# Seven half-size block products in place of eight, for 18 of 22 tile pairs of two up projections

## What is computed

```python
h = x
h = h + 0.5 * swiglu(rms_norm(h, ffn1_norm), w_gate1, w_up1, w_down1)     # FFN 1, "plain"
h = h + mixer(rms_norm(h, mix_norm))          # sparse attention and retention
h = h + 0.5 * swiglu(rms_norm(h, ffn2_norm), w_gate2, w_up2, w_down2)     # FFN 2, "plain"
h = rms_norm(h + sigmoid(rms_norm(h, ple_norm) @ w_ple_gate) * (p @ w_ple_proj), final_norm)
h = h + gated_linear_attention(rms_norm(h, ...))
h = h + conv_ffn(rms_norm(h, ...))            # FFN 3, with a convolution
out = rms_norm(h, final_norm_2)

def swiglu(x, w_gate, w_up, w_down):
    return (silu(x @ w_gate) * (x @ w_up)) @ w_down
```

## Time and profile before

| | us |
|---|---|
| median of 3 runs | 1851.72 (1851.65 to 1852.01) |
| the profiled execution's own time (its span, first to last instruction) | 1849.9 |
| PE busy | 1833.9 (99%) |
| DVE busy | 792.0 (43%) |
| ACT busy | 675.3 (37%) |
| POOL busy | 908.8 (49%) |

### The profile page before, as it was taken

One profiled execution on the slowest core, in us unless ns is written; L12 is line 12 of the kernel. 1 busy time (PEld: TensorE's weight loads), 2 busy tenths in 40 slices (PEclk: granted clock), 3 DMA queues, 4 the chain that ended last, 5 costly groups with the idle time before them and its releaser, 6 DMA issues.

```text
span 1849.9 us, 23884 instructions
## 1 busy us (share of the span) xinstructions
PE 1833.9 (99%) x8616; PEld 1496.0 (81%) x8616; DVE 792.0 (43%) x1301; ACT 675.3 (37%) x927; POOL 908.8 (49%) x710
## 2 busy tenths in 40 slices
PE   9999999999999999999999999999999999999998
PEld 7888888887888668888888888888877888888887
DVE  6222236225775564244222212257655365555312
ACT  5322323232232562234433422246344444444222
POOL 5444455386757424444444444353433454444542
PEclk9999999999999999999999999999999999999999
DMA  5333233253222312232223233232212222223331
GB/s 187 102 102 101 89 100 94 66 157 111 80 80 92 97 46 90 93 102 92 93 100 102 88 94 96 82 122 81 90 58 78 91 95 93 100 92 98 94 96 53
DMA packets 55156, 174.65 MB, mean 94 GB/s; under 512 B 6400, under 2 KB 10752, under 8 KB 55088
## 3 DMA queue, kind: packets, MB, share of 16 engines
q1 hardware_dynamic: 54848, 173.37, 29.4%
q10 hardware_dynamic: 240, 0.36, 0.1%
HBM read 166.63 MB, written 2.10 MB: 91 GB/s over the span
## 4 chain that ended last, share of the span: by engine, by line
PE 98%; DVE 1%; ACT 1%; POOL 0%; issue 0%; DVEq 0%; ACTq 0%; POOLq 0%
PE acc L1666 29%; PE acc L1668 28%; PE acc L1667 28%; PE acc L1771 1%; PE acc L1773 1%; PE acc L1772 1%; PE aux L1965 1%; PE acc L2115 1%; PE acc L2120 1%; PE aux L1947 0%; PE acc L2016 0%; PE aux L1954 0%; PE acc L1784 0%; PE aux L2106 0%; PE acc L1781 0%; PE aux L1995 0%
## 5 line engine op out<-in xcount | busy, mean ns | idle before, releaser
L599 POOL TENSOR_TENSOR w_lo<-w_raw,w_hi 128x512 fp32r<-128x512 f32 x626 | 811.4, 1319 | 903.8 <-ACT w_hi L686 903.8
L1666 PE MATMUL acc<-u_hi,w_lo 128*128 128x512 f32 x1544 | 610.8, 396 | 0.2 <-DVE gcum L1540 0.2
L1668 PE MATMUL acc<-u_hi,w_hi 128*128 128x512 f32 x1544 | 601.2, 389 | 0.0
L1667 PE MATMUL acc<-u_lo,w_hi 128*128 128x512 f32 x1544 | 601.0, 389 | 0.0
L686 ACT ACTIVATE w_hi<-w_raw 128x1024 fp32r<-128x1024 f32 (+2 forms) x313 | 321.9, 1033 | 549.1 <-PE acc L1668 483.9
L1666 PEld LDWEIGHTS acc<-u_hi,w_lo 128*128 128x128 f32 x1544 | 289.9, 188 | 68.8 <-issue 8.6
L1667 PEld LDWEIGHTS acc<-u_lo,w_hi 128*128 128x128 f32 x1544 | 289.9, 188 | 61.7 <-issue 2.6
L1668 PEld LDWEIGHTS acc<-u_hi,w_hi 128*128 128x128 f32 x1544 | 289.8, 188 | 60.9
L1666 PE MATMUL acc<-hid_hi,w_lo 128*128 128x512 f32 (+1 forms) x550 | 209.6, 381 | 0.0
L1667 PE MATMUL acc<-hid_lo,w_hi 128*128 128x512 f32 (+1 forms) x550 | 209.3, 380 | 0.0
L1668 PE MATMUL acc<-hid_hi,w_hi 128*128 128x512 f32 (+1 forms) x550 | 209.3, 380 | 0.0
(11 more groups left out here) (342 smaller groups left out, 2101.8 us busy)
## 6 DMA issues: line engine op xcount, KB each, us to landing
w_raw<-in_w_up SPq DMA_DIRECT2D x132, 512.0 KB, 3.5
w_raw<-in_w_mix SPq DMA_DIRECT2D x67, 512.0 KB, 3.8
w_raw<-in_w_down SPq DMA_DIRECT2D x48, 512.0 KB, 3.5
w_raw<-in_w_gla SPq DMA_DIRECT2D x30, 512.0 KB, 3.3
...
```

Of the source, the lines that this page charges most:

```text
L599: ins = pool.tensor_tensor(w_lo[:, slot, part], w_raw[:, slot, part], w_hi[:, slot, part].bitcast(F32), ALU.subtract)
L1666: pe.matmul(o, w_lo[:, slot, columns], x_hi, start=first, stop=False)
L1667: pe.matmul(o, w_hi[:, slot, columns], x_lo, start=False, stop=False)
L1668: return pe.matmul(o, w_hi[:, slot, columns], x_hi, start=False, stop=last)
```

## The change

The matrix product of a pair is seen as a product of two 2 x 2 block matrices. On the weights' side the rows are gate and up (`g`, `u`) and the columns the two halves of the contraction (1, 2). On the inputs' side the rows are the two halves of the contraction and the columns the left and right 256 tokens. Pairs 0 to 3 (`PLAIN`) stay as they were. Pairs 4 to 21 use Strassen's method in Winograd's form with seven block products, named by their weights operand: `g1`, `s2`, `g2`, `s3`, `s1`, `s4`, `u2`. A product is 4 contraction blocks times three matmuls of 256 columns, 12 in all.

- **Inputs**: DVE writes the fully normalized input (`normalize`, sixteen operations of 256), forms combinations (`combine`, four of 1024) and, with ACT, the high and low parts of all seven operands (`split_comb`, seven of 1024 on each), once for each FFN. This stands in DVE's stream between pair 1 and the first period.
- **Weights**: per pair DVE makes four sums `s1` to `s4` in `aux` (`add`) and their low parts (`sum_low`); ACT makes seven high parts of 512 (`unit_hi`); POOL makes the low parts of `g1`, `g2`, `u2`.
- **Outputs**: bank a of a pair takes g1, then s2, s1 and s4 on top of it. ACT copies it after g1, s2 and s1 (`copy_part`, 256 wide), and TensorE waits for each copy before it goes on in the bank. Bank b takes g2, bank c takes s3 and later u2. DVE adds copies and banks (`left_gate`, `right_up`, `left_up`); the right gate half is read by ACT's Silu straight from the bank.
- **Order on TensorE**: g1(p), s4(p-1), u2(p-1), s2(p), g2(p), s3(p), s1(p). `finish` is s4 and u2.
- **Hidden**: the products of pairs 8 to 21 go to `hid_raw` (in the space of `u_hi`, `u_lo`), and their high and low parts are made at the end, in the space of the combinations (`late_hidden`).
- The loops of these stages on all engines become straight code; TensorE now waits block by block for the hidden parts in the first down tile.

The core of the diff; eight columns of indentation are taken off its lines, and semaphores and helpers are left out.

```diff
+PLAIN = 4
+EARLY = 8
+LATE = KF - EARLY
+QUART = KD // 2
+UNIT = QUART * P
+PRODUCTS = ("g1", "s2", "g2", "s3", "s1", "s4", "u2")
...
+    hid_raw = sb("hid_raw", [P, LATE, S], F32, spot)
...
+    early_hi = sb("early_hi", [P, EARLY, S], F32R, region)
+    early_lo = sb("early_lo", [P, EARLY, S], F32R, region)
+    with ExitStack() as inner:
+        comb = sb("comb", [P, len(PRODUCTS), QUART, 2, HALF], F32R, inner)
+    with ExitStack() as inner:
+        comb_raw = sb("comb_raw", [P, len(PRODUCTS), QUART, 2, HALF], F32, inner)
+    with ExitStack() as inner:
+        late_hi = sb("late_hi", [P, LATE, S], F32R, inner)
+        late_lo = sb("late_lo", [P, LATE, S], F32R, inner)
...
+    def load_pairs(f, name, w):
+        for p in range(PLAIN, KF):
+            if p >= PLAIN + 2:
+                sp.wait_ge(sum_made, made_count(f, p - 2, "s4"))
+            load(n0 + 2 * p, w[2 * p])
+            load(n0 + 2 * p + 1, w[2 * p + 1])
...
+    def lo_pairs(f, name):
+        n0 = plan.first[name][0]
+        for p in range(PLAIN, KF):
+            pool.wait_ge(half_hi, pair_no(f, p) + 1)
+            lo_unit(name, p, "g1").then_inc(half_lo, 1)
+            if p > PLAIN:
+                pool.wait_ge(hi_ready, n0 + 2 * p)
+                lo_unit(name, p - 1, "u2").then_inc(lo_ready, 1)
+            pool.wait_ge(hi_ready, n0 + 2 * p + 1)
+            lo_unit(name, p, "g2").then_inc(lo_ready, 1)
...
+        def period(p):
+            more = p + 1 < KF
+            if p > PLAIN:
+                copy_part(p - 1, 3)
+            unit_hi(p, "s1", sum_hi)
+            copy_part(p, 1)
+            if more:
+                unit_hi(p + 1, "g1", half_hi)
+            if p > PLAIN:
+                right_gate(p - 1)
+            unit_hi(p, "s4", sum_hi)
+            unit_hi(p, "u2", hi_ready)
+            if p > PLAIN:
+                act.wait_ge(tile_freed, t0 + 2 * p)
+            copy_part(p, 2)
+            if more:
+                unit_hi(p + 1, "s2", sum_hi)
+                unit_hi(p + 1, "g2", hi_ready)
+            if PLAIN <= p - 1 < EARLY:
+                hidden_hi(p - 1, up_t[:, (p - 1) % 2, :])
+            left_gate(p)
+            if more:
+                unit_hi(p + 1, "s3", sum_hi)
...
+            elif p == PLAIN - 2:
+                plain_pair(p, lambda: (split_comb("g1"), split_comb("s1"), split_comb("s2")),
+                           lambda: (unit_hi(PLAIN, "g1", half_hi), unit_hi(PLAIN, "s2", sum_hi), split_comb("s3")))
+            else:
+                plain_pair(p, lambda: (unit_hi(PLAIN, "g2", hi_ready), unit_hi(PLAIN, "s3", sum_hi), split_comb("g2")),
+                           lambda: (split_comb("s4"), split_comb("u2")))
+        for p in range(PLAIN, KF):
+            period(p)
...
+        for k in range(EARLY, EARLY + 4):
+            late_hidden(k)
+        copy_part(KF - 1, 3)
+        done[0] = d0
+        act.wait_ge(q_done, q_count(f, KF - 1, "s1"))
+        split_slabs(d0 + 2)
+        for k in range(EARLY + 4, EARLY + 8):
+            late_hidden(k)
+        right_gate(KF - 1)
+        for k in range(EARLY + 8, KF - 1):
+            late_hidden(k)
+        split_slabs(d0 + 3)
+        late_hidden(KF - 1)
...
+        def normalize():
+            for c in range(KD):
+                lo, hi = (0, 3) if c < QUART else (2, 5)
+                for half, q in enumerate((lo, hi)):
+                    tok = slice(half * HALF, (half + 1) * HALF)
+                    ins = dve.scalar_tensor_tensor(comb_raw[:, q, c % QUART, 1, :], h[:, c, tok], col(gain, c), rstd[:, tok],
+                                                   ALU.mult, ALU.mult)
+                ins.then_inc(u_normed, 1)
...
+        def combine():
+            dve.wait_ge(u_normed, KD * (f + 1))
+            b11, b12, b21, b22 = (raw_comb(of) for of in ("g1", "s3", "g2", "s4"))
+            dve.tensor_tensor(raw_comb("s1"), b11, b12, ALU.subtract).then_inc(comb_made, 2)
+            dve.wait_ge(comb_made, comb_count(f, "s1"))
+            dve.scalar_tensor_tensor(raw_comb("s2"), raw_comb("s1"), -1.0, b22, ALU.mult, ALU.subtract).then_inc(comb_made, 1)
+            dve.tensor_tensor(raw_comb("s3"), b22, b12, ALU.subtract).then_inc(comb_made, 1)
+            dve.wait_ge(comb_made, comb_count(f, "s2"))
+            dve.scalar_tensor_tensor(raw_comb("u2"), raw_comb("s2"), -1.0, b21, ALU.mult, ALU.subtract).then_inc(comb_made, 3)
...
+        def period(p):
+            more = p + 1 < KF
+            if p > PLAIN:
+                right_up(p - 1)
+            sum_low(p, "s1")
+            if more:
+                sums_loaded(p + 1)
+                add(p + 1, "s3")
+                add(p + 1, "s1")
+            sum_low(p, "s4")
+            if more:
+                add(p + 1, "s2")
+            if p > PLAIN:
+                left_up(p - 1)
+            if more:
+                add(p + 1, "s4")
+            if p > PLAIN:
+                product(p - 1)
+            if PLAIN <= p - 1 < EARLY:
+                hidden_lo(p - 1, up_t[:, (p - 1) % 2, :])
+            if more:
+                sum_low(p + 1, "s2")
+            left_gate(p)
+            if more:
+                sum_low(p + 1, "s3")
...
+        normalize()
+        combine()
+        split_comb("g1")
+        plain_pair(2)
+        split_comb("s1")
+        split_comb("s2")
+        sums_loaded(PLAIN)
+        for of in ("s3", "s1", "s2", "s4"):
+            add(PLAIN, of)
+        sum_low(PLAIN, "s2")
+        split_comb("s3")
+        plain_pair(3)
+        sum_low(PLAIN, "s3")
+        for of in ("g2", "s4", "u2"):
+            split_comb(of)
+        for p in range(PLAIN, KF):
+            period(p)
+        late_hidden(EARLY)
+        late_hidden(EARLY + 1)
+        right_up(KF - 1)
+        for k in range(EARLY + 2, EARLY + 6):
+            late_hidden(k)
...
+            o = acc[:, bank_of(name, p, part), 0:HALF]
+            for b in range(QUART):
+                columns = slice(at.start + b * P, at.start + (b + 1) * P)
+                pe.matmul(o, w_lo[:, slot, columns], comb[:, q, b, 0, :], start=first and b == 0, stop=False, skip_group_check=not first)
+                pe.matmul(o, w_hi[:, slot, columns], comb[:, q, b, 1, :], start=False, stop=False, skip_group_check=not first)
+                ins = pe.matmul(o, w_hi[:, slot, columns], comb[:, q, b, 0, :], start=False, stop=b == QUART - 1, skip_group_check=not first)
+            return ins
...
+        def finish(p):
+            pe.wait_ge(part_copied, part_count(f, p, 3))
+            multiply(p, "s4", "a", False).then_inc(tile_done, 1)
+            pe.wait_ge(right_ready, pair_no(f, p) + 1)
+            multiply(p, "u2", "c", False).then_inc(tile_done, 1)
+        for p in range(PLAIN, KF):
+            if p < PLAIN + 2:
+                pe.wait_ge(tile_freed, t0 + 2 * PLAIN - BANKS + p - PLAIN + 1)
+            else:
+                pe.wait_ge(gate_act, GATES_FFN[f] + p - 1)
+            multiply(p, "g1", "a", True).then_inc(q_done, 1)
+            if p > PLAIN:
+                finish(p - 1)
+            pe.wait_ge(part_copied, part_count(f, p, 1))
+            multiply(p, "s2", "a", False).then_inc(q_done, 1)
+            pe.wait_ge(tile_freed, t0 + 2 * p - 1)
+            multiply(p, "g2", "b", True).then_inc(q_done, 1)
+            pe.wait_ge(tile_freed, t0 + 2 * p)
+            multiply(p, "s3", "c", True).then_inc(q_done, 1)
+            pe.wait_ge(part_copied, part_count(f, p, 2))
+            multiply(p, "s1", "a", False).then_inc(q_done, 1)
+        finish(KF - 1)
```

291 lines of the change are left out of this document (224 added, 67 removed).

## The result

The changed kernel takes 1874.09 us (median, 1874.03 to 1875.11); the kernel before took 1851.87 us (1851.65 to 1852.61) beside it. The ratio is 1.0121 with a 95% interval of 1.0106 to 1.0135. Forecast were 1865 us and a range of 1849 to 1879: sign and range held, and the loss is 22.2 us where 13.5 were summed.

The account below looks back on a forecast made before the run. TensorE, busy 99% of 1849.9 us, was taken as the bound. Matmuls -28.8, entry +19.1 and +13.4, early periods +6.8, exit +3.0 gave +13.5: median 1851.7 becomes 1865.2 us, range 1849 to 1879.

Parts of the forecast that it names:

- Term 1: Matmuls of the changed pairs: 0.80 us gained per pair, 28.8 us for 2 x 18 pairs.
- Term 2: Entry into the products at pair 4: TensorE waits on DVE's chain, late 19.1 us in FFN 1, 13.4 in FFN 2.
- s2(4) at 63.9: Entry in FFN 1: TensorE starts product s2 of pair 4 at 63.9 us, after DVE's low part of s2.
- Term 3: Pairs 5 to 8: s4 waits 0.85 us for ACT's third copy, four times per FFN, 6.8 us; later periods nothing.
- Term 4: Exit into the down projection: waits for the last copy and the first slab, 1.5 us per FFN, 3 together.
- the fourteen late hidden parts: no wait: Down projection: DVE takes 0.6 us per late part, TensorE 0.68 per step with eight ready, so no wait.
- A: Rival, faster: a much cheaper entry into the products, under 20.4 us for both FFNs; chance 0.12.
- B: Rival, same: costs at their lower bounds, entry 24.9 us, sum +0.8, 1852.5 us; chance 0.11.
- C: Rival, slower still: the 13 late periods each also lose 0.4 to 0.9 us, 17 more, 1882 us; chance 0.10.
- D: Rival, clock: idling at the entry drops TensorE to 1.2 GHz; products after s4(4) cost 6 us, 1871 us; chance 0.17.

Follow-up runs that it names:

- e6: The changed kernel with the normalization as eight DVE operations of 512 elements in place of sixteen of 256: 1871.82 us.
- e2: The changed kernel with ACT's first copy of bank a of pair 4 moved ahead of the work for pair 3: 1877.13 us.
- e3: The changed kernel with high and low parts of the hidden of pairs 4 to 7 moved behind left_gate and the s3 parts: 1866.19 us.
- e1: The changed kernel plus 72 unread 256-column matmuls per FFN between g1(4) and s2(4), where TensorE stood idle: 1874.95 us.

## Why the prediction was right in sign, and short by 9 us

The sum was +13.5 and the spans differ by +22.3. Terms 2, 3 and 4 were short by 4.1, 1.3 and 2.2 us, and 1.2 us were not in the sum at all (0.27 at the start of the program, 0.96 at a late hidden part). No error of one term was made good by another; the range held because it was wide on this side.

**Term 1 held.** -28.8 us, by the late periods of exactly 10.08 us, which is 0.120 us for each of 84 matmuls. The earlier trace rows carried it. The Trainium skill, "TensorE: Matmul & The Clock Gate", Back-to-back issue gap, gives its formula for an isolated matmul; for this stream, with weights changed at each one, its spacing of 109.2 ns and the 42.7 us estimated from it do not hold, and the measured spacing decides.

**Term 2 had the right mechanism and was 4.1 us short** (36.55 for 32.5). Of the 21.3 us in FFN 1, 17.4 are idle (6.34, 10.10 and 0.91); most of the rest is half clock. Two steps of the term were off. First, the rates on DVE. The normalization, forecast "to 47.3", ended at 49.2. DVE's rows, after pair 1:

```profile
40.69 8.48 DVE L1327 SCALAR_TENSOR_TENSOR comb_raw<-h,cols,rstd 128x256 f32<-128x256 f32 x16
49.28 1.23 DVE L1335 TENSOR_TENSOR comb_raw<-comb_raw 128x1024 f32<-128x1024 f32 x1
50.54 1.22 DVE L1337 SCALAR_TENSOR_TENSOR comb_raw<-comb_raw 128x1024 f32<-128x1024 f32 x1
...
58.47 3.43 DVE L1345 TENSOR_TENSOR comb<-comb_raw,comb 128x1024 fp32r<-128x1024 f32 x2
...
71.38 4.58 DVE L1345 TENSOR_TENSOR comb<-comb_raw,comb 128x1024 fp32r<-128x1024 f32 x3
...
81.59 0.41 DVE L1371 TENSOR_TENSOR tmp<-acc,tmp 128x256 f32<-128x256 f32 x1
```

One normalization takes 0.53 us on average. Two shorter stretches give the parts, the first two of the sixteen beside POOL, and four with POOL idle:

```profile
40.69 1.90 DVE L1327 SCALAR_TENSOR_TENSOR comb_raw<-h,cols,rstd 128x256 f32<-128x256 f32 x2
...
45.54 1.66 DVE L1327 SCALAR_TENSOR_TENSOR comb_raw<-h,cols,rstd 128x256 f32<-128x256 f32 x4
```

That is about 0.9 and 0.41 us each, where 0.75 and 0.33 were assumed, from one row of 256 and the slowing of one row of 512. The estimate of 1.22 us for 1024, which no row showed, was exact. The splits of 71.38 took 4.58 us for three where 3.5 were forecast, as POOL worked beside them from 73.38 to 77.10. left_gate, from which s4(4) is released by way of ACT's third copy, ended at 82.0 where 79.3 was forecast. Before it the forecast counted seven operations of 512 behind the low part of s1, and there are six (76.48 to 81.68): a small miscount that by luck paid for slowing and waits there. e6 shows that such microseconds arrive at s4(4) one to one.

Second, **the step "s2(4) at 63.9" failed**: it started at 72.84. I had traced s2(4) on DVE alone, and not on ACT, whose first copy of bank a stands behind the high part of pair 3's hidden and the splits of s4 and u2:

```profile
69.51 0.63 ACT L854 ACTIVATE early_hi<-tmp 128x512 fp32r<-128x512 f32 x1 [0.76 <-DVE tmp L1308]
70.04 1.99 ACT L883 ACTIVATE comb<-comb_raw 128x1024 fp32r<-128x1024 f32 x2
71.94 0.58 ACT L878 ACTIVATE w_hi<-aux 128x512 fp32r<-128x512 f32 x1
72.41 0.37 ACT L888 ACTIVATE tmp<-acc 128x256 f32<-128x256 f32 x1
```

So the profile has one idle of 10.1 us where two shorter ones were forecast (4 at s2 and 5.6 at g2). By e2 this miss cost nothing in time, because s4(4) waits for DVE's chain anyway.

**Term 3 was 1.3 us short** (8.1 for 6.8): 1.01 us a period for 0.85. The order of the steps was the forecast one, and e3 removes just these waits; one low part of the hidden beside POOL took 1.37 us, where 1.1 was assumed. The late periods cost nothing, as said.

**Term 4 was 2.2 us short** (5.2 for 3.0). ACT split the slab as forecast, 0.5 us after s1(21), but POOL's low part took 3.46 us for the forecast 2.6, beside the late hidden parts on DVE:

```profile
258.99 3.46 POOL L708 TENSOR_TENSOR w_lo<-w_raw,w_hi 128x512 fp32r<-128x512 f32 x2 [4.77 <-ACT w_hi L815]
```

and the rest of the difference, about 0.2 us in each FFN, is hand-overs (262.45 to 262.71 from POOL to TensorE). TensorE had the slab 5.4 us after s1(21), not 4.3, with the wait at s4(21) inside it. And "the fourteen late hidden parts: no wait" failed in FFN 2, where eight of them lasted 13.14 us beside POOL and one was late by 0.96 with its gap.

**The rivals.** A needed an entry under 20.4 us and B one near 24.9; it was 36.5. C's late periods did not happen. D did in part: the clock fell, as the last section shows, and as I had written most of it lay in the shadow of DVE's chain; by e1 it cost nothing here. D's price of 6 us for products after s4(4) was wrong for the changed kernel, since its last wait before s4(4) is only 0.91 us; e2, where that wait is 3.1, shows such a price, about half as large (3 us for both FFNs). That 1874 lies near D's 1871 is chance.
